# Inverse of the RWKV scores grown over all four 64x64 tiles, a bank for each row half

## The chip, the cores and the metric

The kernel runs on one core of one Trainium2 chip. The metric is the device time of one execution in microseconds (us). Before the change it is 1620.95 us, the median of three runs (1620.62 to 1621.21).

## The reference

Two layers of a hybrid decoder run over 256 prompt tokens and 64 sample tokens (8 sequences of 8). Each layer is a SwiGLU feed-forward block, a mixer of an RWKV-7 part (8 heads of 64) beside an mLSTM part (4 heads of 128), and a second feed-forward block, with a layer norm after each. The change is in the RWKV-7 part, whose step for one token is

```
def step(S, inp):
    r_t, w_t, k_t, v_t, kk_t, a_t = inp
    sa = jnp.einsum('bhvk,bhk->bhv', S, -kk_t)
    S = (S * w_t[:, :, None, :] + sa[..., None] * (kk_t * a_t)[:, :, None, :]
         + v_t[..., None] * k_t[:, :, None, :])
    return S, jnp.einsum('bhvk,bhk->bhv', S, r_t)
```

The kernel does this in chunks of 64 tokens. Inside a chunk the states depend on each other through a strictly triangular 64x64 matrix of scores for each head, and what is needed is the inverse of one plus that matrix. It then stands between the right-hand side and the vectors `u` that update the state and give the outputs.

## The kernel before

There are NCH = 5 chunks (4 of the prompt, 1 of all samples) and 8 heads. Heads lie in pairs: NJ = 4 pairs, of which one head is on partitions 0 to 63 and the other on 64 to 127 (`PART[0]`, `PART[1]`). A 64x64 matmul uses one of four tiles of TensorE, given by the row half its operands lie on and the half (columns of the array) its output goes to. A pair that stays on its half uses the two straight tiles; one that goes from `PART[q]` to `PART[1 - q]` uses the two crossed ones.

The inverse of a chunk is grown by doubling. `ati` holds one plus the scores. Level 0 masks it (on VectorE, into `xti` directly) and `first_growth` turns that into `xi`; TensorE then holds the inverse X and its transpose in `xx`, which lies in the space of `z`. Each later level of each chunk is one step n of a loop of NSTEP = 27 steps (six levels for a prompt chunk, three for the samples; the list `LEVELS` goes through the chunks level by level). Step n has four parts on three engines:

- `product(n)` on TensorE (L681): `ati` times X, 8 matmuls, into bank 0 or 1.
- VectorE (L1569): the product times the level's mask, into `t1`.
- `grow(n)` on TensorE, emitted one step later, after `product(n + 1)`: X times that (L693, 8 matmuls, not at a chunk's last level) and its transpose (L697, 8 matmuls), both into bank 2 or 3 by n, side by side. It waits for `t1`, and for the copy of the growth two back, which had the same bank.
- `copy_growth(n)` on ScalarE (L1073): the growth from its bank to `xx`, 128x512, or 128x256 where only one half is made.

These steps are the skeleton on which the rest of the mixer hangs. In steps of fixed numbers TensorE also does side work through bank 7 (`side`, with ScalarE's `copy_side`, each waiting for the one before): values (L627, copied at L1050), keys (L636, L643, copied at L1053, L1056), states (L656). It also does the mLSTM tiles: `tile_scores` in steps 9 and 14 (L527, L530), `tile_values` in steps 7 and 12 (L549 to L553), heads of the samples in steps 17 to 20 (L562 to L571), and left-overs from step 21 (L592, L428, L601). The order on every engine is written out by hand. Behind the loop, `recurrence` goes through the four prompt chunks with X transposed (L807), the products with the state (L794, L831) and the samples between. GpSimd makes a masked copy of the samples' keys for each pair in `memory_term` (L1741) for `samples_memory_after` (L775, L779); one of the four outputs lies in the gaps that `xx` leaves after the loop.

A fp32 matmul shows as two records in the trace, each with its weight load (PEld). The ends of matmul records are modelled; starts are what rests on firm ground.

## Time and profile before

| | |
|---|---|
| median of three runs | 1620.95 us |
| the profiled execution's own time | 1628.67 us |
| its span, from first to last instruction | 1626.9 us |
| PE busy | 1538.8 us, 95% |
| DVE, ACT, POOL busy | 845.4, 675.8, 373.9 us |
| mean granted clock | 0.965 |
| level loop of layer 0 | 399.4 to 488.9 us |
| level loop of layer 1 | 1201.0 to 1284.2 us |

PE is TensorE with its matmuls and PEld its weight loads, DVE is VectorE, ACT ScalarE, POOL GpSimd, SP the engine that issues DMAs. The granted clock is a share of 2.4 GHz; 0.50 is 1.2 GHz. In an order of time each row is a merged group: start, duration, engine, line, operation, output and inputs, shape, count, and in brackets how long the engine was idle before it and what ended that. "Issue" there is idle time for which the profile shows no release.

### The profile page before, as it was taken

The page shows a single profiled execution, that of the slowest core. Times are in us where ns is not written, and L with a number is a line of the kernel's source. Part 1 is how long each engine was busy: PE and PEld are TensorE (multiplying, and loading weights), DVE is VectorE, ACT ScalarE, POOL GpSimd, SP SyncE. Part 2 cuts the span into 40 slices and gives each one's busy share as a digit, 9 for nine tenths or more (in the row PEclk, how much of TensorE's full clock was granted, in tenths as well). Part 3 has the DMA queues.
Part 4 walks back from the last instruction along what each step waited for, and adds up shares of the span by engine and source line. Part 5 has one row for each costly group of instructions (what it writes and reads, how often), then busy time and mean ns, then how long its engine had stood idle before and what let it go on. Part 6 is the DMA issues. An engine that isn't in the chain of part 4 may idle for free.

```text
span 1626.9 us, 34539 instructions
## 1 busy us (share of the span) xinstructions
PE 1538.8 (95%) x13754; PEld 1478.2 (91%) x13754; DVE 845.4 (52%) x1333; ACT 675.8 (42%) x1111; POOL 373.9 (23%) x382
## 2 busy tenths in 40 slices
PE   7999998999998899999899999989999988999995
PEld 7999997998877899999899999979989777999994
DVE  4444345686265754444364443366954576444343
ACT  4333336656322453333353333367653245333332
POOL 6222460013112422221212221100131313222110
PEclk9999999999897999999999999999999899999998
DMA  7454542442112545454445454524430433545430
GB/s 204 144 154 143 166 146 79 125 112 77 29 44 73 173 131 153 145 151 143 135 117 154 144 153 156 142 79 117 104 81 3 116 97 112 169 145 154 144 115 33
DMA packets 307943, 197.73 MB, mean 122 GB/s; under 512 B 7616, under 2 KB 283104, under 8 KB 307840
## 3 DMA queue, kind: packets, MB, share of 16 engines
q1 hardware_dynamic: 304224, 189.64, 40.3%
q0 software_dynamic: 3616, 6.62, 1.6%
q8 instruction: 76, 1.25, 0.3%
q14 instruction: 27, 0.22, 0.0%
HBM read 187.46 MB, written 8.78 MB: 121 GB/s over the span
## 4 chain that ended last, share of the span: by engine, by line
PE 87%; DVE 5%; ACT 3%; DVEq 2%; issue 1%; POOL 1%; DMA 0%; ACTq 0%; SPq 0%; POOLq 0%
PE bank L1917 24%; PE bank L1918 23%; PE bank L1919 23%; PE bank L681 1%; PE bank L697 1%; PE bank L1960 1%; PE bank L592 1%; ACT x L2145 1%; PE bank L693 1%; DVEq L2284 1%; PE bank L568 1%; POOL xl L2387 1%; PE bank L429 1%; DVE xl L2275 1%; PE bank L1997 1%
## 5 line engine op out<-in xcount | busy, mean ns | idle before, releaser
L2243 DVE TENSOR_TENSOR wlo<-raw,whi 128x1024 fp32r<-128x1024 f32 x340 | 426.2, 1256 | 414.7 <-ACT whi L2121 413.5
L1917 PE MATMUL bank<-xh,whi 128*128 128x320 f32 x1896 | 591.3, 312 | 11.0 <-DVE wlo L2243 9.7
L2121 ACT ACTIVATE whi<-raw 128x1024 fp32r<-128x1024 f32 x340 | 359.0, 1059 | 571.3 <-PE bank L1919 565.8
L1918 PE MATMUL bank<-xl,whi 128*128 128x320 f32 x1896 | 588.0, 310 | 0.0
L1919 PE MATMUL bank<-xh,wlo 128*128 128x320 f32 x1896 | 587.9, 310 | 0.0
L1917 PEld LDWEIGHTS bank<-xh,whi 128*128 128x128 f32 x1896 | 357.7, 189 | 16.2 <-issue 6.2
L1918 PEld LDWEIGHTS bank<-xl,whi 128*128 128x128 f32 x1896 | 357.9, 189 | 0.5
L1919 PEld LDWEIGHTS bank<-xh,wlo 128*128 128x128 f32 x1896 | 357.8, 189 | 0.0
L2397 POOL TENSOR_TENSOR hl<-scratch,hh 128x320 f32 x88 | 146.6, 1666 | 529.1 <-DVE scratch L2308 529.1
L1917 PE MATMUL bank<-hh,whi 128*128 (+1 forms) x704 | 218.6, 310 | 0.7 <-ACT vec L2163 0.7
L1919 PE MATMUL bank<-hh,wlo 128*128 (+1 forms) x704 | 217.4, 309 | 0.0
L1918 PE MATMUL bank<-hl,whi 128*128 (+1 forms) x704 | 217.4, 309 | 0.0
L1917 PEld LDWEIGHTS bank<-hh,whi 128*128 128x128 f32 x704 | 132.3, 188 | 1.3 <-ACT vec L2163 1.0
L1918 PEld LDWEIGHTS bank<-hl,whi 128*128 128x128 f32 x704 | 132.3, 188 | 0.3
L1919 PEld LDWEIGHTS bank<-hh,wlo 128*128 128x128 f32 x704 | 132.3, 188 | 0.0
L2307 DVE TENSOR_TENSOR hh<-scratch,bank 128x320 f32 (+1 forms) x88 | 42.8, 487 | 122.5 <-PE bank L1919 121.0
L397 POOL TENSOR_TENSOR gbias<-ones 1x1 f32<-1x1 f32 x10 | 11.9, 1193 | 281.6 <-DVE scratch L1211 134.5
L1073 ACT ACTIVATE z<-bank 128x512 f32<-128x512 f32 (+1 forms) x54 | 27.8, 515 | 96.4 <-PE bank L697 96.4
L1960 PE MATMUL bank<-xh,whi 128*128 128x320 f32 x120 | 42.3, 360 | 26.9 <-ACT xh L2142 26.9
L1960 PEld LDWEIGHTS bank<-xh,whi 128*128 128x128 f32 x120 | 27.5, 229 | 28.6 <-issue 28.6
L2126 ACT ACTIVATE scratch<-z 128x320 f32<-128x320 f32 x48 | 20.4, 469 | 53.9 <-DVE z L2251 53.9
L2308 DVE TENSOR_TENSOR scratch<-scratch,bank 128x320 f32<-128x320 f32 x88 | 42.2, 479 | 0.0
(370 smaller groups left out, 1689.3 us busy)
## 6 DMA issues: line engine op xcount, KB each, us to landing
raw<-in_ffn_wg SPq DMA_DIRECT2D x88, 512.0 KB, 3.8
raw<-in_ffn_wu SPq DMA_DIRECT2D x88, 512.0 KB, 3.8
raw<-in_ffn_wd SPq DMA_DIRECT2D x88, 512.0 KB, 3.6
raw<-in_w_in SPq DMA_DIRECT2D x60, 512.0 KB, 3.8
raw<-in_w_out SPq DMA_DIRECT2D x16, 512.0 KB, 5.9
raw<-in_state_C SPq DMA_DIRECT2D x8, 512.0 KB, 6.0
out_s_C<-raw SPq DMA_DIRECT2D x8, 512.0 KB, 3.3
ring<-in_state_wkv POOLq DMA_DIRECT2D x2, 1024.0 KB, 8.7
```

Source lines behind the costliest of these rows:

```text
L429: return pe.matmul(out, src, ident[0:rows, 0:rows], start=True, stop=True)
L1073: act.activation(xx[:, c, lo:hi, :, :].rearrange("p x j s -> p (x j s)"), bank[2 + n % 2][:, lo * NJ * CH:hi * NJ * CH], ACT.Copy).then_in ...
L1917: pe.matmul(out, w_hi, hi, start=start, stop=False)
L1918: pe.matmul(out, w_hi, lo, start=False, stop=False)
L1919: return pe.matmul(out, w_lo, hi, start=False, stop=stop)
L1960: pe.matmul(outs[n], w[:, slot, k * P:(k + 1) * P], xh[:, k, :], start=(k == 0 and w is whi), stop=False)
L2121: act.activation(whi[:, slot, :], raw[:, slot, :], ACT.Copy).then_inc(hi_ready.sem, 1)
L2126: act.activation(sq[:, o, :], z[:, o, :], ACT.Square).then_inc(sq_ready.sem, 1)
L2243: dve.tensor_tensor(wlo[:, slot, :], raw[:, slot, :], whi[:, slot, :].bitcast(F32), ALU.subtract).then_inc(lo_ready.sem, 1)
L2307: dve.tensor_tensor(out, silu[:, s, :], bank[d % RS][:, 0:T], ALU.mult)
L2308: dve.tensor_tensor(hval[:, s, :], silu[:, s, :], bank[d % RS][:, 0:T], ALU.mult).then_inc(up_done.sem, 1)
L2397: pool.tensor_tensor(at(hl), hval[:, k % 2, :], at(hh).bitcast(F32), ALU.subtract).then_inc(hl_done.sem, 1)
```

## The change

The product now goes crossed, from the row half of the head to the other half (`PART[1 - q]`), so `t1` lies on the other half, and there the transposed inverse is kept too: `xi(q, c, j)` is on `PART[q]`, `xti(q, c, j)` on `PART[1 - q]`. A growth of both takes all four tiles: X goes crossed back, the transpose stays straight. What comes from row half 1 goes to bank 2, what comes from row half 0 to bank 3, at every level, so that `grow(n)` waits for the copy of growth n - 1. `first_growth` makes both X and its transpose, 16 matmuls in place of 8, and alternates between banks 2, 3 and banks 0, 1; the first product waits for the copy of growth 3. `copy_growth` takes two activations, one for each bank and head. What works with the transposed inverse in the recurrence takes its right-hand side on the other half, so the products that make it go crossed, and the side product RV goes straight. `memory_term` is two operations for each pair, and the output that lay in the gaps of `xx` has areas of its own.

```diff
-        xi, xti = xx[:, :, 0, :, :], xx[:, :, 1, :, :]
+        def xi(q, c, j):
+            return xx[PART[q], c, q, j, :]
+
+        def xti(q, c, j):
+            return xx[PART[1 - q], c, q, j, :]
...
-                        for q, part in enumerate(PART):
+                        for q in range(2):
                             at = (n * NJ + j) * NA
-                            last = pe.matmul(b[part, at:at + NA], scores[PART[1 - q], c, j, q, 0, :],
+                            last = pe.matmul(b[PART[1 - q], at:at + NA], scores[PART[1 - q], c, j, q, 0, :],
                                              uv[PART[1 - q], c, j, q, :], start=True, stop=True)
...
+        def growth_bank(n):
+            return 2 * ((n + 1) % 2) if n < NCH else 2
+
         def first_growth(pe, L, c):
 
             pe.wait_ge(t1_ready.sem, t1_ready.by(L, c + 1))
             if c >= 2:
                 pe.wait_ge(x_copied.sem, x_copied.by(L, c - 1))
             for j in range(NJ):
-                for part in PART:
-                    last = pe.matmul(bank[2 + c % 2][part, j * CH:(j + 1) * CH], xti[part, c, j, :],
-                                     ident[part, part], start=True, stop=True)
+                for q, part in enumerate(PART):
+                    pe.matmul(bank[growth_bank(c) + q][part, j * CH:(j + 1) * CH], t1[part, c, j, :], ident[part, part],
+                              start=True, stop=True)
+                for q, part in enumerate(PART):
+                    last = pe.matmul(bank[growth_bank(c) + q][PART[1 - q], j * CH:(j + 1) * CH], ident[part, part],
+                                     t1[part, c, j, :], start=True, stop=True)
             last.then_inc(x_mm.sem, 1)
 
         def product(pe, L, n):
 
             lv, c = LEVELS[n]
-            pe.wait_ge(x_copied.sem, x_copied.by(L, LEVELS.index((lv - 1, c)) + 1))
+            pe.wait_ge(x_copied.sem, x_copied.by(L, max(LEVELS.index((lv - 1, c)) + 1, NCH - 1)))
             pe.wait_ge(t1_ready.sem, t1_ready.by(L, n - 1))
             for j in range(NJ):
-                for part in PART:
-                    last = pe.matmul(bank[n % 2][part, j * CH:(j + 1) * CH], ati[part, c, j, :], xi[part, c, j, :],
+                for q, part in enumerate(PART):
+                    last = pe.matmul(bank[n % 2][PART[1 - q], j * CH:(j + 1) * CH], ati[part, c, j, :], xi(q, c, j),
                                      start=True, stop=True)
             last.then_inc(t1_mm.sem, 1)
...
             pe.wait_ge(t1_ready.sem, t1_ready.by(L, n + 1))
-            pe.wait_ge(x_copied.sem, x_copied.by(L, n - 1))
-            if lv < NLV[c] - 1:
-                for j in range(NJ):
-                    for part in PART:
-                        pe.matmul(bank[2 + n % 2][part, j * CH:(j + 1) * CH], xti[part, c, j, :], t1[part, c, j, :],
+            pe.wait_ge(x_copied.sem, x_copied.by(L, n))
+            for j in range(NJ):
+                if lv < NLV[c] - 1:
+                    for q in range(2):
+                        pe.matmul(bank[2 + q][PART[q], j * CH:(j + 1) * CH], xti(q, c, j), t1[PART[1 - q], c, j, :],
                                   start=True, stop=True)
-            for j in range(NJ):
-                for part in PART:
-                    last = pe.matmul(bank[2 + n % 2][part, (NJ + j) * CH:(NJ + j + 1) * CH], t1[part, c, j, :],
-                                     xti[part, c, j, :], start=True, stop=True)
+                for q in range(2):
+                    last = pe.matmul(bank[2 + q][PART[1 - q], j * CH:(j + 1) * CH], t1[PART[1 - q], c, j, :],
+                                     xti(q, c, j), start=True, stop=True)
             last.then_inc(x_mm.sem, 1)
...
             act.wait_ge(x_mm.sem, x_mm.by(L, n + 1))
-            lo, hi = int(lv == NLV[c] - 1), 1 + int(lv > 0)
-            act.activation(xx[:, c, lo:hi, :, :].rearrange("p x j s -> p (x j s)"),
-                           bank[2 + n % 2][:, lo * NJ * CH:hi * NJ * CH], ACT.Copy).then_inc(x_copied.sem, 1)
+            for q in range(2):
+                rows = slice(0, P) if lv < NLV[c] - 1 else PART[1 - q]
+                last = act.activation(xx[rows, c, q, :, :].rearrange("p j s -> p (j s)"), 
+                                      bank[growth_bank(n) + q][rows, 0:NJ * CH], ACT.Copy)
+            last.then_inc(x_copied.sem, 1)
...
-            if j == 1:
...
+            own = bcast(bmask[:, :].rearrange("p (b o) -> p b o", o=1), 2, NA)
+            for q in range(2):
+                src = bcast(bkt[NPC][:, j, q:q + 1, :], 1, SB)
+                last = pool.tensor_tensor(bktm[j][q], src, own, ALU.mult)
+            last.then_inc(memory_terms.sem, 1)
```

## Rows read from the trace of the kernel before

**Rows 1.** The page, busy time by engine.

```profile
PE 1538.8 (95%) x13754; PEld 1478.2 (91%) x13754; DVE 845.4 (52%) x1333; ACT 675.8 (42%) x1111; POOL 373.9 (23%) x382
```

**Rows 2.** Busy time by stretch: length, PE, PEld, DVE, ACT, POOL, clock, DMA share, GB/s.

```profile
399.40:488.90 89.50, 83.14 (x1709) 73.47 (x1707) 38.43 (x118) 32.77 (x76) 20.77 (x17) 0.90 0.14 36
1201.00:1284.20 83.20, 77.11 (x1709) 67.87 (x1707) 38.45 (x118) 32.74 (x77) 20.78 (x17) 0.98 0.15 39
...
421.00:423.00 2.00, 2.00 (x9) 1.78 (x9) 0.00 (x0) 0.00 (x0) 0.00 (x0) 0.50 0.00 0
```

**Rows 3.** PE in order of time, growth 6 of layer 1 (two tiles).

```profile
1212.04 0.63 PE L693 MATMUL bank<-spare,z 64*64 64x64 f32 x16
1212.50 0.63 PE L697 MATMUL bank<-z,spare 64*64 64x64 f32 x16
```

**Rows 4.** The scores: one group in order of time, and the line's durations (min/median/max).

```profile
388.36 1.10 PE L712 MATMUL bank<-scratch 64*64 64x128 f32 x32
...
L712 PE MATMUL bank<-scratch x320: 269/269/321, 388.4 to 1198.7; 64*64 64x128 f32 x160
```

**Rows 5.** PE in order of time, values (crossed) and first growth (straight), layer 1.

```profile
1203.63 0.51 PE L627 MATMUL bank<-ident,scratch 64*64 64x64 f32 x10 [0.99 <-ACT ring L1046]
1203.92 0.27 PE L670 MATMUL bank<-ident,z 64*64 64x64 f32 x2
1203.97 0.28 PE L627 MATMUL bank<-ident,scratch 64*64 64x64 f32 x3
...
1204.10 0.51 PE L670 MATMUL bank<-ident,z 64*64 64x64 f32 x11
```

**Rows 6.** Groups by line and shape, 395 to 520 us: count, busy, mean ns, idle before.

```profile
L1073 ACT ACTIVATE z<-bank 128x512 f32<-128x512 f32 x17 | 10.1, 597 | 39.0 <-PE bank L697 39.0
...
L1073 ACT ACTIVATE z<-bank 128x256 f32<-128x256 f32 x10 | 3.8, 375 | 11.5 <-PE bank L697 11.5
```

**Rows 7.** ACT in order of time in steps 5 and 6, and PE's L549 of step 7.

```profile
1211.74 0.77 ACT L1050 ACTIVATE scratch<-bank 64x256 f32<-64x256 f32 x2
1212.41 0.58 ACT L1073 ACTIVATE z<-bank 128x512 f32<-128x512 f32 x1
1213.18 0.60 ACT L1073 ACTIVATE z<-bank 128x512 f32<-128x512 f32 x1 [0.19 <-PE bank L697]
...
1213.07 1.16 PE L549 MATMUL bank<-ring 128*128 128x129 f32 x8
```

**Rows 8.** PE in order of time, the tile scores of step 9.

```profile
1218.93 2.02 PE L527 MATMUL bank<-scratch,sel 4*128 4x128 f32 x16 [0.41 <-DVE scratch L1352]
```

**Rows 9.** In order of time: the copy of growth 10 (ACT), and L549 of step 12.

```profile
1225.48 0.60 ACT L1073 ACTIVATE z<-bank 128x512 f32<-128x512 f32 x1 [0.99 <-PE bank L697]
...
1228.47 0.49 PE L549 MATMUL bank<-ring 128*128 128x129 f32 x2 [0.37 <-DVE ring L1339]
```

**Rows 10.** In order of time: L527 of step 14, and the copy of growth 15.

```profile
1235.46 1.97 PE L527 MATMUL bank<-scratch,sel 4*128 4x64 f32 x16 [0.24 <-DVE scratch L1354]
...
1241.02 0.60 ACT L1073 ACTIVATE z<-bank 128x512 f32<-128x512 f32 x1 [1.01 <-PE bank L697]
```

**Rows 11.** In order of time: the copy of growth 19, and L592 of step 21.

```profile
1255.83 0.60 ACT L1073 ACTIVATE z<-bank 128x512 f32<-128x512 f32 x1 [3.06 <-PE bank L697]
...
1261.91 1.95 PE L592 MATMUL bank<-spare,ring 64*128 64x512 f32 x4 [1.41 <-POOL spare L1729]
```

**Rows 12.** PE in order of time, growth 21 of layer 1.

```profile
1264.70 1.06 PE L693 MATMUL bank<-spare,z 64*64 64x64 f32 x16
1265.55 1.06 PE L697 MATMUL bank<-z,spare 64*64 64x64 f32 x16
```

**Rows 13.** PE in order of time, the first product of the recurrence.

```profile
1284.59 0.68 PE L807 MATMUL bank<-scratch,z 64*64 64x64 f32 x16 [0.48 <-ACT z L1073]
```

**Rows 14.** PE in order of time, inside growth 8 of layer 0.

```profile
418.25 0.38 PE L697 MATMUL bank<-z,spare 64*64 64x64 f32 x5 [1.17 <-issue]
```

**Rows 15.** PE in order of time, matmuls of 16 columns in the recurrence.

```profile
1287.51 3.99 PE L737 MATMUL bank<-scratch 64*64 64x16 f32 x128
```

More of the change, by code:

```diff
@@ L246, in hymba_kernel, with by_head @@
         decay = area(10504, SB, NJ, NA)
-        gaps = zflat.rearrange("p (c x r) -> p c x r", c=NCH, x=2)[:, 0:SB // 2, 0, :]
-        bktm_out = [area(2560, SB, P, of=spare), gaps.rearrange("p c (b n) -> p c b n", b=2),
-                    area(0, SB, P, of=spare), area(15304, SB, P)]
-        bktm = [[t[..., q * NA:(q + 1) * NA] for q in range(2)] for t in bktm_out]
+        def by_head(t):
+            return [t[..., q * NA:(q + 1) * NA] for q in range(2)]
+        bktm = [by_head(area(2560, SB, P, of=spare)), [area(20424, SB, NA), area(4314, SB, NA)],
+                by_head(area(0, SB, P, of=spare)), by_head(area(15304, SB, P))]
         wkv_out = area(5384, SB, NJ, NA)
@@ L744, in samples_r @@
             for j in range(NJ):
-                for part in PART:
-                    last = pe.matmul(bank[3][part, j * NA:(j + 1) * NA], s0sum[part, j, 0, :], ident[part, part],
-                                     start=True, stop=True)
+                for q, part in enumerate(PART):
+                    last = pe.matmul(bank[3][PART[1 - q], j * NA:(j + 1) * NA], s0sum[part, j, 0, :],
+                                     ident[part, part], start=True, stop=True)
             last.then_inc(samples_mm.sem, 1)
@@ L753, in samples_u @@
             for j in range(NJ):
-                for part in PART:
-                    last = pe.matmul(bank[3][part, j * NA:(j + 1) * NA], xti[part, NPC, j, :], rsb_s[part, j, :],
+                for q, part in enumerate(PART):
+                    last = pe.matmul(bank[3][part, j * NA:(j + 1) * NA], xti(q, NPC, j), rsb_s[PART[1 - q], j, :],
                                      start=True, stop=True)
@@ L792, in recurrence @@
                     for j in range(NJ):
-                        for part in PART:
-                            last = pe.matmul(bank[0][part, j * NA:(j + 1) * NA], ar[part, j, c, 0, :],
+                        for q, part in enumerate(PART):
+                            last = pe.matmul(bank[0][PART[1 - q], j * NA:(j + 1) * NA], ar[part, j, c, 0, :],
                                              state[part, c % 2, j, :], start=True, stop=True)
@@ L805, in recurrence @@
                 for j in range(NJ):
-                    for part in PART:
-                        last = pe.matmul(bank[1][part, j * NA:(j + 1) * NA], xti[part, c, j, :], rhs[part, j, :],
+                    for q, part in enumerate(PART):
+                        last = pe.matmul(bank[1][part, j * NA:(j + 1) * NA], xti(q, c, j), rhs[PART[1 - q], j, :],
                                          start=True, stop=True)
@@ L1562, in vector_mixers @@
                     dve.wait_ge(ati_ready.sem, ati_ready.by(L, c))
-                    tt(xti[:, c - 1, :, :], ati[:, c - 1, :, :], level_mask(0), ALU.mult).then_inc(t1_ready.sem, 1)
+                    tt(t1[:, c - 1, :, :], ati[:, c - 1, :, :], level_mask(0), ALU.mult).then_inc(t1_ready.sem, 1)
             for n in range(NCH, NSTEP):
@@ L1732, in memory_term @@
         def memory_term(pool, L, j):
-            if j == 1:
-                own = bcast(bmask[:, 0:SB].rearrange("p (c b o) -> p c b o", b=2, o=1), 3, P)
-                src = bkt[NPC][:, j, :, :].rearrange("p (o u q) n -> p o u (q n)", o=1, u=1)
-                src = bcast(bcast(src, 1, SB // 2), 2, 2)
-            else:
-                own = bcast(bmask[:, :].rearrange("p (b o) -> p b o", o=1), 2, P)
-                src = bcast(bkt[NPC][:, j, :, :].rearrange("p (o q) n -> p o (q n)", o=1), 1, SB)
-            pool.tensor_tensor(bktm_out[j], src, own, ALU.mult).then_inc(memory_terms.sem, 1)
+            own = bcast(bmask[:, :].rearrange("p (b o) -> p b o", o=1), 2, NA)
[3 more added lines that the diff above has]
+            last.then_inc(memory_terms.sem, 1)
         def pool_mixers(pool, L):
```

## The prediction

> **What bounds the kernel now.** I read the page first: TensorE (PE) is busy for 95% of the span [rows 1]. The change touches only one stage, so next I read the stretches of that stage, the level loop, once in each layer: 89.5 us in layer 0 and 83.2 us in layer 1, PE busy 93% in both, ACT 33 us and DVE 38 us [rows 2]. The same 27 steps take 6.3 us more in layer 0; the granted clock says why, 0.90 against 0.98, and a row inside layer 0 stands at 0.50, the 1.2 GHz level [rows 2]. The change of time is to be found in about 173 us of 1626.9, and at most what the grow groups take there. Third, I followed both loops in order of time, and wrote down at every idle piece of PE who released it. PE works through each step without a gap until it meets a wait that another engine ends: these places decide how much of a faster group is kept.
>
> **What a group costs.** With two tiles, a group of 8 fp32 matmuls of 64x64 leaves 16 records and its successor starts 0.47 us later, 29 ns a record [rows 3]. A full growth is two such groups, 0.93 us (L693 and L697); there are 17 of these in a layer (steps 5 to 13 and 15 to 22), and 5 last ones with one group.
>
> **Removed and added on PE.** The 17 full growths keep their 16 matmuls, but spread over all four tiles, one bank for each row half. Is that faster? The same layout runs in the scores at L712: 32 records of 128 columns in 1.10 us, one of them 0.269 us, so (1.10 - 0.27) / 31 = 27 ns a record, with four tiles of 107 ns each [rows 4]. Twice as many columns at the pace of two tiles: there four tiles do work twice as fast. With 64 columns the trace has only a short case: L627 (the crossed tiles) and L670 (the straight ones) follow each other, and L670 begins 0.29 us after L627 while 6 records of L627 are still to come; both are over in 0.75 us where 2 x 0.47 = 0.93 stood for two tiles, and in the overlapped piece some 11 records start in 0.18 us, 16 ns each [rows 5]. So 32 records cost between 32 x 14.5 = 0.46 us (half of 29) and 0.56 us (L627's own rate of 0.29 / 16 = 18 ns, if sending is the limit). I take 0.50, from the 16 ns: a full growth saves 0.43 us, bounds 0.37 to 0.47, where PE sets the time, and twice that at 1.2 GHz. The first growths go from 8 matmuls on two tiles to 16 on four: the same 0.47 to 0.50. Products, samples, recurrence and the RV side change only tiles: counts stay, I take zero; a short overlap with a neighbour, as in rows 5, could bring 0.1 us at each, half a microsecond in all.
>
> **Added on ACT.** One copy of 128x512 took 0.60 us and one of 128x256 0.38 [rows 6]. A full growth is now copied by two of 128x256: 0.77 us, as the pair at L1050 took [rows 7], so +0.17. A last growth goes from one copy (0.38) to two on one row half: +0.39. A first growth from one to two: +0.4. ACT gains 17 x 0.17 + 5 x 0.39 + 5 x 0.4 = 6.8 us a layer, and it has room in total (33 of 83). What counts is where a copy is waited for.
>
> **The added wait.** Growths of the levels no longer alternate between banks 2 and 3: both belong to each one, so the next growth waits for the copy of the one before (before, of the one two back). Behind the waiting growth stand, on PE, its side work, the next product and whatever tile work the step has. L697 of growth 6 starts at 1212.50 and its copy at 1213.18, 0.21 after the 0.47 of the group [rows 3, 7]. So from the end of a growth to the end of its copies it is 0.21 + 0.77, and with an estimated 0.06 for the signal back 1.04 us; the side group and the product between two growths give 0.94 with the clock up. Where a side group stands between, this is nearly hidden (0.1); in steps 6 and 8 there is none, and about 0.55 is waited.
>
> **The sum, layer 1, place by place.** (a) The first copy: L627 waits for L1046, which is behind the copy of growth 0 on ACT [rows 5]: +0.4. (b) Step 6: ACT comes late from its exponents to the copy of growth 5, at 1212.41 [rows 7]. Shifted by 0.4 and 0.77 long it ends at 1213.6; growth 6, which began at 1212.04 without it, now begins at 1213.65 and ends at 1214.15, and L549 starts at 1214.2 and not 1213.07: +1.1. Then growth 7 gains, growth 8 waits, and the next end is DVE's L1352, released by ACT's copy behind growth 7: L527 at 1218.93 [rows 8] becomes 1219.9. So (a) and (b) together: +0.95. (c) Steps 9 to 12: L549 waits for DVE, that for ACT's exponents, these for the copy of growth 10 [rows 9]. Growths 9 and 10 save 0.86, the two longer copies and the new wait take 0.4 back: -0.45; growth 11 gains nothing. (d) Steps 12 to 14: L527 at 1235.46 waits for DVE behind the copy of growth 12 [rows 10]: -0.43 + 0.17 = -0.25. (e) Steps 15 to 17: the copy of growth 15 at 1241.02 releases exponents and side copies [rows 10]; ACT is nearly full there, -0.1. (f) Steps 18 to 20: nothing waits between the long L568 groups, so growths 17, 18 and 19 save 1.29; then copy of growth 19, table load, roots, DVE, Pool and L592 at 1261.91 [rows 11], the copy +0.17: -1.1. DVE's head sums run beside it and end in time. (g) Growth 21 runs at the low clock, each of its groups 0.85 us apart [rows 12]: -0.86; growth 22 at full clock: -0.43. (h) After the last growth L807 waits for its copy [rows 13]: +0.4. Sum: 0.95 - 0.45 - 0.25 - 0.1 - 1.1 - 0.86 - 0.43 + 0.4 = -1.8 us.
>
> **Layer 0** has the same places and two differences. In growth 8 PE stood for 1.17 us with nothing to wait for [rows 14]; the delay of (b) falls into that gap, which is worth 0.9. And growths 9 and 10 ran mostly at 1.2 GHz [rows 2], so (c) is -1.0. Sum -1.8 - 0.9 - 0.55 = -3.3 us.
>
> Pool's four memory terms become two operations of 128x512 for one of 128x1024. PE uses them only in the fourth chunk of the recurrence and after it, behind three chunks of other work: nothing; without that cover it would be about 4 x 0.2 us, what a halved copy cost more on ACT [rows 6, 7]. Nothing else of SP's or Pool's queue moves. Together -5.1 us, so the profiled span goes from 1626.9 to 1621.8. The profiled execution's own time was 1628.67, 7.7 over the median of the runs; I take the same difference from the median: 1620.95 - 5.1 = 1615.8 us.
>
> **A rule that speaks against it.** In the overlap of L627 and L670 tiles of the same row half loaded and multiplied in turns, and each kept its pace [rows 5]. The Trainium skill, "TensorE: Matmul & The Clock Gate", Part 3, The mechanism, says that a weight load overlaps a running matmul only when the row group differs; with it the two tiles of a row half would go one after the other. It is the third rival below; the trace so far disagrees, but over 6 records only.
>
> **Rivals.** First, the clock turns against it. In layer 0 a stretch from 420.7 to 427.4 us stood at half clock (one slice of it is in the rows), and layer 1, at 0.98 in all, had none in those steps [rows 2]. PE does the same work in less time and waits more in steps 6 and 8, so a further stretch of that kind may fall in; 6.7 us at half clock cost 3.3: -5.1 + 3.3 gives 1619, within 0.2%. The same the other way: the stretch of layer 0 goes, -3.3 more and 0.6 less to gain there: 1613. Second, the new wait costs more than I give it, by 0.3 us at each of the 7 neighbouring growths without long work between them, twice: +4.2 gives 1620, no change. Third, the one that ends slower: four tiles go no faster than two with 64 columns, because loading or sending 30 ns a record is the floor. For it speaks L737, whose matmuls have 16 columns and not 64, and which still took 3.99 us for 128 records, 31 ns each [rows 15]; that is a floor for each tile (61 ns) or for all of them, and the row does not tell which. Against it speak rows 4 only in part (27 ns is also just what 128 columns need) and rows 5. Then a growth stays at 0.93 and only costs are left: (b) +1.8, (c) +0.4, (d) +0.2, (e) +0.3, (f) +0.2, (h) +0.4, 3.3 in layer 1, and 0.9 less in layer 0: 5.7, which gives 1626.6. From 1615.8 that is 10.8 us, the 0.43 of some 25 growths' worth on the path (12 in layer 1, 13 in layer 0, one at half clock counted twice). So it decides from 5.1 / 25 = 0.20 us a growth, 32 x 6.4 ns: above 22 ns a record nothing is gained.
>
> **How the numbers follow.** Forecast 1615.8 with its own range 1613.5 to 1618 (0.37 or 0.47 for each of the 25 is 1.5 up or 1.0 down, the small overlaps 1 down, layer 0's gap 0.9 up): 0.40. Clock in its favour: 0.12. Clock against: 0.22. Wait dearer: 0.12. Four tiles no faster: 0.14. A measurement of this kernel can tell about 0.2% (3.2 us) from no change, so faster means under 1617.7. Forecast (nine tenths of it) and good clock give 0.48 + 0.02 from the rest; slower is the third rival and a little of a bad clock: 0.16; same: 0.34. The range leaves out most of the third rival and the ends of the clock cases: 1611.5 to 1622.
>
> **What would show it.** The growth lines: 32 records in 0.6 to 0.7 us at full clock with the next group 0.50 us after the start, not 0.93. L1073 twice as often, 128x256. A wait of PE for L1073 before growths 6 and 8, about 0.5 us each. L549 of step 7 a good 1 us later counted from the first L627; L592 about 1.2 earlier than without that. The wait before L807 0.4 longer. The two level loops together 5 us shorter, everything behind them as before. It is wrong if the records of a growth start 27 to 30 ns apart, or if the clock row of the loops differs by more than 0.03 from 0.90 and 0.98.

## The result

The changed kernel took 1629.1 us in the median of 18 executions (1618.4 to 1632.6), the kernel before 1622.3 (1620.6 to 1625.4, 18 executions): a ratio of 1.0034, interval 1.0023 to 1.0044. It is slower, by about a third of a per cent, where 5 us less had been forecast, and it lies above the range. Two things stand beside this from the start. The spread became three times as wide (14 us for 5), and the time follows the mean granted clock: from 1618.4 us at 0.969 to 1632.6 at 0.956. The first profiled execution was by chance the fastest of the 18; a second profile, of a repeat of the same kernel, is a typical one at 1628.8 us. Both are needed: the first shows what the change does where the clock is at 2.4 GHz, the second what it costs. The kernel before was repeated and profiled again too; that profile, 1619.25 us, is 2.6 under the median of its repeat.

| | before, rows of the section above | before, repeated | after, first profile | after, repeated |
|---|---|---|---|---|
| profiled execution, us | 1628.67 | 1619.25 | 1618.43 | 1628.84 |
| span, us | 1626.9 | 1617.5 | 1616.7 | 1627.1 |
| mean granted clock | 0.965 | 0.972 | 0.969 | 0.959 |

The page of the changed kernel, first profile: busy time by engine, and the copies of the growths. PE has lost 15 us of busy time against [rows 1] (part of it clock), ACT has gained 8.

```profile
PE 1523.3 (94%) x13914; PEld 1461.7 (90%) x13914; DVE 844.6 (52%) x1333; ACT 684.2 (42%) x1165; POOL 376.3 (23%) x390
...
L1085 ACT ACTIVATE z<-bank 128x256 f32<-128x256 f32 (+1 forms) x108 | 36.3, 379 | 81.2 <-PE bank L708 80.9
```

**What a growth costs now.** PE in order of time, first profile, layer 1, step 19: a product (L693), growth 18 (L705 straight, L708 crossed) and the head sums behind it. This answers to [rows 3].

```profile
1238.47 0.33 PE L693 MATMUL bank<-z,spare 64*64 64x64 f32 x4
...
1238.64 0.46 PE L693 MATMUL bank<-z,spare 64*64 64x64 f32 x10
1238.89 0.27 PE L708 MATMUL bank<-z,spare 64*64 64x64 f32 x2
1238.93 0.23 PE L693 MATMUL bank<-z,spare 64*64 64x64 f32 x2
1238.99 0.22 PE L705 MATMUL bank<-spare,z 64*64 64x64 f32 x2
1239.00 0.23 PE L708 MATMUL bank<-z,spare 64*64 64x64 f32 x2
1239.05 0.23 PE L705 MATMUL bank<-spare,z 64*64 64x64 f32 x2
...
1239.40 0.68 PE L642 MATMUL bank<-ident,spare 64*64 64x64 f32 x16
```

Two records of L705 and two of L708 start every 0.055 to 0.06 us, about 14.5 ns each, and the whole of product and growth takes 1239.40 - 1238.47 = 0.93 us, the time that a growth alone took. With 0.46 for the product the growth is 0.47: the better end of my bounds, 0.46 to 0.56.

**What PE waits for.** The same view, layer 1, the waits of the stage that bear on the sum; they answer to [rows 5, 8, 9, 10, 11, 13].

```profile
1196.04 0.51 PE L633 MATMUL bank<-ident,scratch 64*64 64x64 f32 x10 [1.24 <-ACT ring L1057]
...
1205.60 0.27 PE L705 MATMUL bank<-spare,z 64*64 64x64 f32 x2 [1.28 <-ACT z L1085]
...
1210.25 0.27 PE L705 MATMUL bank<-spare,z 64*64 64x64 f32 x2 [0.42 <-ACT z L1085]
...
1211.73 0.46 PE L533 MATMUL bank<-scratch,sel 4*128 4x128 f32 x2 [0.32 <-DVE scratch L1365]
...
1221.99 0.49 PE L555 MATMUL bank<-ring 128*128 128x129 f32 x2 [0.37 <-DVE ring L1352]
...
1228.62 1.63 PE L533 MATMUL bank<-scratch,sel 4*128 4x64 f32 x13 [0.29 <-DVE scratch L1367]
...
1253.15 1.95 PE L598 MATMUL bank<-spare,ring 64*128 64x512 f32 x4 [1.95 <-POOL spare L1742]
...
1273.30 1.01 PE L818 MATMUL bank<-scratch,z 64*64 64x64 f32 x13 [0.87 <-ACT z L1085]
```

Two waits are new, before growths 6 and 8 (1.28 and 0.42 us, both for the copy of the growth before), and three have grown: before the first values 1.24 for 0.99 [rows 5], before the first left-over group 1.95 for 1.41 [rows 11], before the first product of the recurrence 0.87 for 0.48 [rows 13].

**Where the time went.** The stage cut at these instructions. The us at half clock of a stretch (its time at the 1.2 GHz level) are 2 x (1 - granted clock) x its length. "Clock up" is a stretch without any: for before from its repeat (the last full-clock one, 21.24, from a version described below), for after from the first profile, from the layer that had none. The last row has half clock in every profile, given behind its lengths.

| stretch | before, clock up | after, clock up | difference | after, repeated, layer 1 (us at half clock) |
|---|---|---|---|---|
| first values to L549/L555 of step 7 | 9.44 | 10.19 | +0.75 | 10.18 (0) |
| to the tile scores of step 9 | 5.86 | 5.50 | -0.36 | 5.50 (0) |
| to L549/L555 of step 12 | 9.54 | 8.87 | -0.67 | 10.22 (3.5) |
| to the tile scores of step 14 | 6.99 | 6.63 | -0.36 | 6.64 (0) |
| to the first left-over group | 26.45 | 24.53 | -1.92 | 25.32 (3.5) |
| to the first product of the recurrence | 21.24 | 20.15 | -1.09 | 24.74 (10.4) |
| to the first matmul of the next stage | (40.69, 13.8 low) | (40.92, 13.9 low) | +0.2 | 41.72 (16.7) |

With +0.25 ahead of the first values, a layer is 3.4 us shorter as long as the clock is up, nearly twice what I had expected (1.8). The last column is what a typical execution makes of it. Three stretches of layer 1 (the level loop from the first values up to the left-overs, from there to the recurrence, the recurrence) in both repeats; columns: length, PE, PEld, DVE, ACT, POOL, granted clock, DMA share, GB/s. First the kernel before:

```profile
1194.15:1252.43 58.28, 53.28 (x1305) 50.50 (x1305) 21.74 (x60) 24.84 (x57) 13.04 (x13) 1.00 0.09 22
1252.43:1275.13 22.70, 22.22 (x370) 16.18 (x371) 15.50 (x54) 5.64 (x13) 5.50 (x3) 0.92 0.31 90
1275.13:1315.82 40.69, 34.67 (x731) 29.17 (x731) 25.69 (x60) 10.93 (x22) 9.91 (x9) 0.83 0.26 72
```

The changed kernel:

```profile
1201.12:1258.98 57.86, 51.05 (x1353) 47.56 (x1353) 21.42 (x59) 27.52 (x77) 12.77 (x13) 0.94 0.10 22
1258.98:1283.72 24.74, 23.87 (x370) 16.32 (x371) 15.62 (x54) 7.16 (x19) 5.50 (x3) 0.79 0.28 82
1283.72:1325.44 41.72, 35.23 (x731) 29.43 (x731) 24.79 (x60) 10.93 (x22) 10.68 (x13) 0.80 0.26 71
...
1262.00:1264.00 2.00, 2.00 (x37) 1.50 (x30) 0.60 (x3) 0.98 (x4) 1.00 (x1) 0.50 0.03 8
```

PE has the same 370 records in the middle stretch, with 10.4 us at 1.2 GHz for 3.6. The first profile has this stretch with the clock up throughout:

```profile
1253.15:1273.30 20.15, 19.28 (x371) 13.42 (x371) 15.49 (x54) 7.16 (x19) 5.52 (x3) 1.00 0.35 100
```

So here 10.4 us at half clock cost 24.74 - 20.15 = 4.6 us, 0.44 us for each. Over a whole execution the second profile of after has 2 x 0.041 x 1627 = 133 us at half clock, the first 100; that of before, repeated, has 2 x 0.028 x 1617.5 = 91, and its first one 114. So two executions of one kernel give a price over the whole program: 10.4 us of span for 33 us at half clock in the changed kernel, 9.4 for 23 in the kernel before, 0.3 to 0.4 us for each.

### The profile page after: what moved, and what is told of

Its sections match the earlier page's. It is cut to its first block, busy times and chain, and to the rows that moved or that the text cites. A ratio compares the mean times of both kernels' runs of the same rounds, so it can differ in the third digit from the quotient of the medians.

```text
span 1616.7 us, 34921 instructions
## 1 busy us (share of the span) xinstructions
PE 1523.3 (94%) x13914; PEld 1461.7 (90%) x13914; DVE 844.6 (52%) x1333; ACT 684.2 (42%) x1165; POOL 376.3 (23%) x390
## 4 chain that ended last, share of the span: by engine, by line
PE 87%; DVE 5%; ACT 4%; DVEq 2%; issue 1%; POOL 1%; DMA 0%; ACTq 0%; POOLq 0%
PE bank L1927 24%; PE bank L1928 24%; PE bank L1929 24%; PE bank L1970 1%; PE bank L693 1%; PE bank L598 1%; ACT x L2155 1%; DVEq L2294 1%; PE bank L574 1%; PE bank L705 1%; POOL xl L2397 1%; PE bank L435 1%; DVE xl L2285 1%; PE bank L2007 1%; DVE z L2276 1%
## 5 line engine op out<-in xcount | busy, mean ns | idle before, releaser
L1085 ACT ACTIVATE z<-bank 128x256 f32<-128x256 f32 (+1 forms) x108 | 36.3, 379 | 81.2 <-PE bank L708 80.9
```

The lines of the kernel that those rows point to most:

```text
L1085: last = act.activation(xx[rows, c, q, :, :].rearrange("p j s -> p (j s)"), bank[growth_bank(n) + q][rows, 0:NJ * CH], ACT.Copy)
```

## The experiments

The theory after the first profile: the change does what it should at full clock, but it makes PE's idle pieces in this stage longer, more of the stage then runs at 1.2 GHz, and this takes more than the growths give. The rival: the waits and copies cost it by themselves. All versions ran beside the kernel before, whose median was 1623.4, 1622.2 and 1623.0 us in the three groups of four.

**The two kernels again.**

> The changed kernel again, unaltered, with the kernel before on the same chip. Clock theory (the level loops got shorter, but more of the execution runs at 1.2 GHz): its executions spread from about 1618 to 1632 us in step with their mean granted clock, about 1.2 us for each 0.001; at equal clock it lies some 5 us under the kernel before; a profile of a slow execution shows level loops of 77 to 80 us where the clock is up, and stretches at 0.50 that the fast one hasn't. Cost theory (the bank wait and the longer copies cost more than the tiles give): the time does not follow the clock, and slow executions have longer waits of PE for L1085 at full clock.

> The kernel before as a run of its own, for its clock beside its times. Clock theory: its executions stand at 0.963 to 0.966 and 1620.5 to 1626 us, and a change of clock moves it by the same 1.2 us for each 0.001. Cost theory: the clock is that of the changed kernel, and the times differ all the same.

After: 1628.9 us (1620.4 to 1634.4, 12 executions), ratio 1.0031 (1.0012 to 1.0051). Before: 1621.9, ratio 0.9998 (0.9986 to 1.0010). The loss is real, and what this measurement tells apart is about 0.2%. Of the 12 executions of after the nine at a clock of 0.962 or less took 1626 to 1634 us, the other three, at 0.964 to 0.968, 1620.4 to 1621.8. The kernel before stood at 0.966 to 0.973, higher than I had written. At nearly equal clock the changed kernel is ahead, as the clock theory has it: its six executions at 0.964 and 0.965 took 1620.4 to 1624.7 us, the five of the kernel before at 0.966 took 1625.0 to 1628.6 (all runs together). The mean clock does not fix the time alone: at 0.971 the kernel before took from 1620.3 to 1625.1 us.

**The growth without the turns.** The changed kernel, all straight matmuls of a growth sent ahead of the crossed ones (the expectation has the two the other way round; the edit is this one):

```
-            for j in range(NJ):
-                if lv < NLV[c] - 1:
+            if lv < NLV[c] - 1:
+                for j in range(NJ):
                     for q in range(2):
                         pe.matmul(bank[2 + q][PART[q], ...
+            for j in range(NJ):
                 for q in range(2):
                     last = pe.matmul(bank[2 + q][PART[1 - q], ...
```

> Changed kernel, but in a growth the crossed half (8 matmuls) is sent as a whole before the straight half, as before the change; layout, banks, waits and copies stay. Clock theory: the growth takes 0.8 to 0.93 us again, each level loop is 3 to 5 us longer at full clock, PE is busier and the granted clock steadier, near 0.965: about 1625. Cost theory: 8 to 10 us slower than the changed kernel, about 1638, since only costs are left. Prediction's pace theory (four tiles no faster than two): no change from the changed kernel.

1629.9 us, ratio 1.0051 (1.0034 to 1.0067): 5 us over what the clock theory gave and 8 under the cost theory, so neither number came. PE in order of time, layer 1, a growth with the clock up:

```profile
1243.29 0.51 PE L705 MATMUL bank<-spare,z 64*64 64x64 f32 x10
1243.58 0.27 PE L709 MATMUL bank<-z,spare 64*64 64x64 f32 x2
1243.60 0.28 PE L705 MATMUL bank<-spare,z 64*64 64x64 f32 x3
```

Alone, ten records of L705 take 0.29 us, 29 ns each; the crossed ones start only then, as in [rows 5]. Stretches with one full growth at full clock (to the tile scores of steps 9 and 14) are 5.76 and 6.89 us for 5.50 and 6.63, so a growth comes to 0.73 us here and not 0.47: the turns are worth 0.26 us each, an estimated 34 times 0.26 = 8.8 us of PE time over both layers. The median moved by 1 us, the ratio by 0.2%, and the intervals overlap. Most of PE's gain is therefore not in the result. A place where it goes stands in the same trace: the slower growths bring PE later to the first left-over group, and it waits 1.51 us there, not 1.95; behind it the clock stays up (the same in layer 0, 20.81 us at 1.00):

```profile
1262.61 1.95 PE L598 MATMUL bank<-spare,ring 64*128 64x512 f32 x4 [1.51 <-POOL spare L1743]
```

```profile
1262.61:1283.40 20.79, 19.92 (x370) 14.06 (x371) 15.49 (x54) 7.15 (x19) 5.51 (x3) 1.00 0.34 97
```

Some of the gained time turns into idle time of PE there. In the second profile of the changed kernel the wait that is 0.44 us longer stands ahead of a stretch that is 4 us longer, by its half clock. The length of the wait alone does not decide this: 1.95 us were followed by none in the first profile of the changed kernel, and the shorter 1.41 us of the kernel before by 3.4 us at half clock in each layer of both its profiles. And this version has its half clock elsewhere: 2 x 0.035 x 1625.9 = 114 us in all, of which 7 (layer 0) and 10 (layer 1) lie between the first values and the tile scores of step 14, where the second profile of the changed kernel has 7 and 3.4.

**The costs without the gain.** The kernel before, with the changed kernel's wait and its copies in two activations, and then with the copies alone. The full edit:

```
-            pe.wait_ge(x_copied.sem, x_copied.by(L, n - 1))
+            pe.wait_ge(x_copied.sem, x_copied.by(L, n))
 ...
-            act.activation(xx[:, c, lo:hi, :, :]..., bank[2 + n % 2][:, lo * NJ * CH:hi * NJ * CH], ACT.Copy)
+            for q in range(2):
+                x0, x1, rows = (q, q + 1, slice(0, P)) if hi - lo == 2 else (lo, hi, PART[q])
+                last = act.activation(xx[rows, c, x0:x1, :, :]..., 
+                                      bank[2 + n % 2][rows, x0 * NJ * CH:x1 * NJ * CH], ACT.Copy)
```

> Kernel before, with the two costs alone: a growth waits for the copy of the growth just before it, and each copy is two activations. Clock theory: +2 to +3 us a layer by the sum (wait in steps 6 and 8, later exponents, later u), about 1627, with the clock within 0.002 of before. Cost theory: +5 us a layer and more, 1632 and up.

> The kernel before with each growth's copy in two activations, but with the wait of before (for the copy of two growths back). The version with the new wait as well was at 1640.9 us, 1.012 of before. Theory (the wait carries most of the loss when growths are not faster): 1624 to 1630 us, so that the wait alone is 11 us or more. Rival (ScalarE's longer copies carry it): 1634 us or more.

Both together: 1640.9 us, ratio 1.0117 (1.0098 to 1.0135), 4 executions; the clock theory had said 1627, the cost theory 1632 and more. The copies alone: 1633.9, ratio 1.0077 (1.0058 to 1.0095), also 4, at the edge of what the rival asked for, where I had said 1624 to 1630. In both the rival's number held and mine did not: the copies carry some 12 us and the wait some 7, where my ledger had the costs of both at 5.7 us together. What remained to settle is by what way they cost so much. The copies alone are the clearest case, since they hardly lengthen anything by themselves. Groups by line and shape of that version, 395 to 520 us, where its copies stand in both shapes:

```profile
L1075 ACT ACTIVATE z<-bank 128x256 f32<-128x256 f32 x34 | 11.2, 382 | 36.1 <-PE bank L697 36.0
L1075 ACT ACTIVATE z<-bank 64x256 f32<-64x256 f32 x20 | 7.5, 375 | 10.7 <-PE bank L697 10.6
```

ACT in order of time, one such pair:

```profile
1214.70 0.66 ACT L1075 ACTIVATE z<-bank 128x256 f32<-128x256 f32 x2 [1.09 <-PE bank L697]
```

A pair of 128x256 is over in 0.66 us where one 128x512 took 0.60 [rows 6], and a first or last copy (two of 64 rows) in 0.76 for 0.38. In its profile the stretch from the first scores to the start of the next stage is 140.4 and 141.5 us in the two layers, against 135.3 in both of the kernel before: 11.3 of the 13.6 us by which the two spans differ. Pieces with equal half clock show the copies' own cost: ahead of the first values 14.19 us for 13.66, from step 12 to 14 7.05 for 6.99, from there to the left-overs 26.57 for 26.45, from these to the recurrence 23.06 for 22.70 (some 3.4 us at half clock in both), 1.1 us a layer. And 27 and 31 us of these stretches are at half clock, against 17 and 17: 24 us more, which at 0.3 to 0.44 are 7 to 11 of the 11.3. The first values waited 1.52 us for 0.99 there, and in layer 1 10.2 us at half clock followed, where before had none:

```profile
1202.09 0.51 PE L627 MATMUL bank<-ident,scratch 64*64 64x64 f32 x10 [1.52 <-ACT ring L1046]
```

So the two theories were not as separate as I had put them: the copies do cost 12 us, and most of it by way of the clock. The version with both costs shows how loosely a single wait and the clock hang together: in its profile L592 waits 1.48 us in both layers, and the stretch behind is 27.83 us at 0.75 in layer 0 and 23.08 at 0.93 in layer 1. Against this version the changed kernel is 12 us faster (1640.9 to 1628.9), which the new layout as a whole brings; the turns alone brought 1 to 3 of it.

**Filling one idle piece.** The changed kernel with four matmuls that nobody reads, just ahead of the first left-over group:

```
+        def filler(pe, b, times):
+            for _ in range(times):
+                pe.matmul(b[:, 0:4 * CH], ident[:, :], lvmask[:, 0:4, :], start=True, stop=True)
 ...
+                if n == LEFT_AT[0]:
+                    filler(pe, bank[(n - 1) % 2], 4)
```

> The changed kernel with four matmuls more in each layer, 128x128 by 256 columns, sent to an idle bank just before the first left-over group (L598), where TensorE stood idle for 1.95 us; their result is overwritten and never read, so they are extra work of about 1.7 us laid into that idle piece. Theory (the change is faster at full clock, and loses by longer stretches at half clock that follow its idle pieces): the 10.4 us at half clock between L598 and the first samples group L818 go, that stretch falls from 24.8 to between 20.2 and 22 us in each layer, and the whole comes to 1620 to 1624 us against 1629 without the extra matmuls. Rival (the added costs are the waits and copies themselves, and the clock falls elsewhere anyway): no gain, 1629 or up to 1632 us, with the stretch still at 24 us or the same time at half clock found in its neighbours.

1618.0 us (1614.9 to 1621.0, 11 executions), ratio 0.9972 (0.9960 to 0.9983): 11 us less than the changed kernel (by the ratios 10), for 8 x 0.43 = 3.4 us of extra work (two records a matmul, one started every 0.216 us). PE in order of time, layer 1:

```profile
1253.15 0.63 PE L649 MATMUL bank<-scratch 64*64 64x64 f32 x16
1253.71 1.99 PE L868 MATMUL bank<-lvmask,ident 128*128 128x256 f32 x8
1255.73 1.95 PE L598 MATMUL bank<-spare,ring 64*128 64x512 f32 x4
```

The piece of 1.95 us is filled (L868 stands as 8 records for 4 matmuls), L598 begins no later (6.14 us behind the copy of growth 19 in both versions), and the stretch behind it is as short as in the fastest execution, at full clock:

```profile
1255.73:1275.89 20.16, 19.29 (x371) 13.42 (x371) 15.50 (x54) 7.14 (x19) 5.51 (x3) 1.00 0.36 100
```

The time is better than the 1620 to 1624 expected. Twice 4.6 us are these stretches; the remaining 1.7 of the 11 I can't place.

**The same on the kernel before** (three matmuls ahead of L592).

> The kernel before with three such extra matmuls at the same place (idle there 1.41 us), results never read. It tells whether the extra matmuls are worth something by themselves. Theory: in the kernel before the stretch from L592 to L807 has only 3.4 us at half clock in each layer, so at most 1.8 us a layer is to be had: 0 to -3.5 us. If it gains as much here as on the changed kernel, what they give is not a debt of the change.

1619.4 us, ratio 0.9985 (0.9973 to 0.9996): 2.8 us less. The stretch fell from 22.70 to 21.24 in each layer and had nothing at half clock, the value used in the table above. The same cure brings four times as much on the changed kernel, so most of what it brings there, 8 of the 11 us, is a debt of the change.

**The control.** The same four matmuls on the changed kernel, two steps earlier, where PE has no idle piece (`if n == LEFT_AT[0] - 2`).

> A control: the changed kernel with the same four extra unread matmuls a layer as in the version that came to 1618.0 us, but two steps earlier, where TensorE has no idle piece. Theory (they help only where they fill an idle piece): no gain, 1629 to 1633 us, their own 1.7 us a layer being added. Rival (any extra work there holds the clock up): under 1625 us.

1632.5 us, ratio 1.0043 (1.0023 to 1.0062). PE in order of time, layer 1:

```profile
1263.14 1.09 PE L598 MATMUL bank<-spare,ring 64*128 64x512 f32 x2 [1.95 <-POOL spare L1749]
```

The stretch from there to the recurrence:

```profile
1263.14:1287.88 24.74, 23.87 (x370) 16.29 (x371) 15.61 (x54) 7.16 (x19) 5.50 (x3) 0.79 0.29 82
```

The wait of 1.95 us is there as in the changed kernel, and behind it the same 24.74 us at 0.79; in layer 0 it is 26.37 us at 0.74. Extra work alone gains nothing here and adds its own length; the gain needs it in the idle piece. Four of its 10 executions, at 0.964 to 0.968, took 1622.4 to 1625.8 us, the other six 1632.3 to 1636.2: the spread of the changed kernel is still there, while the 11 executions with the piece filled lie within about 6 us.

**More fillings**: two and one ahead of growths 6 and 8, two ahead of the recurrence's first product, four ahead of the samples' solution (L766), on top of the four; and for comparison the kernel before with three ahead of L592 and the two and the four in the recurrence.

```
+                    if n in (NCH + 2, NCH + 4):
+                        pe.wait_ge(t1_ready.sem, t1_ready.by(L, n))
+                        filler(pe, bank[(n - 1) % 2], 2 if n == NCH + 2 else 1)
 ...
                 if c == 0:
+                    filler(pe, bank[1], 2)
 ...
                     if c == 2:
+                        filler(pe, bank[7], 4)
                         samples_u(pe, L)
```

> warm21 with more of the same extra matmuls where the changed kernel waits or stands idle: two before growth 7's neighbour in the first level, one two steps later, two ahead of the first solution of the recurrence, four before the samples' solution; none is read. Theory: the time at half clock in the level loop and in the recurrence falls too, 1612 to 1619 us. Rival (each extra matmul delays the wait's end or the work behind it, since the pieces are only 0.4 to 1.3 us long): 1620 to 1628 us, slower than warm21.

> The kernel before with extra unread matmuls in the same places as the changed kernel's best version as far as it has them: three ahead of L592, two ahead of L807, four ahead of the samples' solution. It tells what the grow groups are worth with the idle pieces of both kernels filled. Theory: 1614 to 1618 us, so that the changed kernel (1616.0) is ahead by 0 to 2 us only. If it comes to 1620 or more, the change is worth over 4 us once its clock is held.

1616.0 us, ratio 0.9963 (0.9949 to 0.9977), and 1618.1, ratio 0.9968 (0.9957 to 0.9979). The second steps brought 2.0 and 1.3 us: most was in the one piece. Over all five versions with the piece filled, the stretch from the left-overs to the recurrence stands at 1.00 in both layers, ten of ten. With both kernels' idle pieces filled the intervals overlap: the change is then worth 2 us by the medians, 1 by the ratios, and not surely anything.

**One copy for both banks.** The changed kernel, with banks laid out in pairs, so that one activation copies both:

```
-            for q in range(2):
-                rows = slice(0, P) if lv < NLV[c] - 1 else PART[1 - q]
-                last = act.activation(xx[rows, c, q, :, :]..., bank[growth_bank(n) + q][rows, 0:NJ * CH], ACT.Copy)
+            last = act.activation(xx[:, c, :, :, :]...,
+                                  pair[growth_bank(n) // 2][:, :].rearrange("p (x r) -> p x r", x=2)[:, :, 0:NJ * CH],
+                                  ACT.Copy)
```

> The changed kernel, but both banks of a growth are copied in one activation (128 rows, two pieces of 256 columns from two neighbouring banks) instead of two. The waits and TensorE's work stay. Theory (the second activation lengthens the waits ahead of growths 6 and 8, of L818 and of the roots before L598, and TensorE's clock falls after them): a copy takes 0.60 us and not 0.77, a last copy and a first one no more than 0.6, the waits before growths 6 and 8 shrink from 1.28 and 0.42 us to about 1.0 and 0.2, and the whole falls by several times the 0.17 us of each place: 1617 to 1624 us against 1629. Rival (the copies cost only their own length where they are waited for, about 0.17 at five places and 0.4 at three, in two layers): -4 us, 1625 to 1627.

> One copy for a growth as in the run before, with the extra unread matmuls of the version that came to 1616.0 us. Theory (both cures act on the same thing, the pieces in which TensorE stands idle, so their gains overlap in part): 1606 to 1614 us, faster than the kernel before and than either cure alone. If it stays at 1616 the single copy gives nothing once the idle pieces are filled.

Alone 1625.5 us (12 executions, 1615.6 to 1627.5), ratio 1.0003 (0.9987 to 1.0020): 3.4 us less than the changed kernel (by the ratios 4.5), the rival's figure and not mine. The copy is 0.59 us long, but the pair had been over in 0.63 to 0.66, so there were only 0.06 us to be had at the waits before the first values, growths 6 and 8 and the left-overs; before the recurrence, where the last copies had taken 0.77, the wait fell from 0.87 to 0.70. Groups of this version by line and shape, 395 to 520 us:

```profile
L1084 ACT ACTIVATE z<-pair 128x512 f32<-128x512 f32 x27 | 16.0, 593 | 45.0 <-PE pair L709 44.9
```

PE in order of time, its wait before the first left-over group:

```profile
1254.23 1.09 PE L599 MATMUL pair<-spare,ring 64*128 64x512 f32 x2 [1.89 <-POOL spare L1742]
```

The idle piece is 1.89 us, and 24.6 us with 10.3 at half clock follow as before. With the fillings as well: 1610.5 us (1608.6 to 1611.7, 6 executions), ratio 0.9922 (0.9910 to 0.9934), the fastest version, 12.5 us under the kernel before, at a clock of 0.975 in its profile. Its level loop and the stretch behind it in layer 1:

```profile
1190.22:1246.52 56.30, 53.38 (x1367) 48.74 (x1367) 21.53 (x59) 26.12 (x57) 12.83 (x13) 0.97 0.10 23
1246.52:1266.80 20.28, 20.28 (x376) 14.10 (x375) 15.50 (x54) 6.39 (x13) 5.78 (x4) 1.00 0.35 101
```

The time lies within the 1606 to 1614 expected. Why one copy gives another 5.5 us on top of the fillings, more than the 3.4 it gives alone, no single place shows; the two profiles differ by 3.1 us.

## Why the prediction was wrong

**The pace of four tiles: right.** 0.47 us for a growth, the better end of the bounds (0.46 to 0.56, 0.50 taken). The third rival (no faster than two tiles) is out; that its 1626.6 us is the number of mine nearest to the result is luck. The Trainium skill says in "TensorE: Matmul & The Clock Gate", Part 3, The mechanism, that a weight load overlaps running matmuls only where the row group differs. This trace disagrees: straight and crossed tiles of one row half take turns at 14.5 ns a record against 29 for two tiles alone, so a row half starts a record every 29 ns, where with two tiles, one in each row half, it started one every 58. They do so only if sent in turns, as the version without turns shows with 0.73 us.

**The copies: the size was off, in their favour, in the ledger.** A pair of 128x256 takes 0.63 to 0.66 us and not the 0.77 I took from a pair of 64 rows; so (a) was +0.25 and not +0.4. Only the last copies, two of 64 rows, took the 0.77. ACT's busy time rose by 8.4 us over both layers, 4.2 a layer, where 6.8 had been added up.

**The places: right in sign, mostly too small.** (a) and (b) to the tile scores of step 9: +0.64 measured (0.25 + 0.75 - 0.36), 0.95 forecast. (c) -0.67 for -0.45; (d) -0.36 for -0.25; (e) and (f) -1.92 for -1.2; (g) and (h) -1.09 at full clock, where the forecast of -0.89 had 0.43 from half clock in it. In all -3.4 us a layer for -1.8 in layer 1. The waits before growths 6 and 8 were forecast at about 0.5 each and were 1.28 and 0.42; that for growth 6 was contained in the start I gave for it (1213.65 - 1203.63 - 0.4 = 9.62 us behind the first values, measured 9.56; for L549 of step 7 10.17, measured 10.19), so "about 0.5" contradicted my own ledger, and (b) itself was right.

**The step that failed: the clock was taken as given.** I priced each wait and each longer copy at its own length and laid the profile's clock over the result. The version with the costs alone measures this step: 5.7 us in my ledger, 18.7 in the medians. The first rival named the right mechanism and the right steps (the waits in steps 6 and 8), but put it at one further stretch of 6.7 us, 3.3 us of time, with a chance of 0.22. In fact the second profile has some 42 us more at half clock than the repeat of the kernel before (133 for 91), nearly all in this stage: in the level loop, behind it and in the recurrence. At 0.3 to 0.44 us each, an estimate from the stretches and spans above, these are 13 to 18 us; the two profiles need 16.4 (6.8 us gained at full clock, 9.6 lost between 1619.25 and 1628.84), the medians 13.7. The kernel before has such executions too: that of the rows had 114 us at half clock, most of the surplus in layer 0, and took 1628.67; in the changed kernel this became the usual case. The sign that I gave, a clock of the loops more than 0.03 from 0.90 and 0.98, did come: cut as in [rows 2], up to the recurrence, they stand at 0.88 and 0.90 in the second profile (86.1 and 85.0 us), against 0.98 in both layers (83.1 us) in the repeat of the kernel before. In the first profile they are 80.2 and 79.7 us at 0.96 and 0.98.

**A sum that hid it.** In (f) I counted 1.1 us of gain ahead of L592, and never asked what becomes of the wait there. The chain of copy, roots, DVE and Pool takes 6.14 us from the copy of growth 19 to L598, for 6.08 before; growth 20 lies beside that chain, so what it saves moves nothing and only brings PE to the wait earlier, and the idle piece grows from 1.41 [rows 11] to 1.95 us. That one piece, filled, gives back 11 us, where the whole loss is 7. A faster engine that still waits for the same chain has a longer idle piece as its first result.

**What stays open.** Which idle piece is followed by half clock is not fixed: in the first profile the same wait of 1.95 us before L598 was followed by 20.15 us at full clock, in both layers, and 1.51 us by none where 1.41 and 1.48 were followed by some. The runs show that filling one such piece, or making the copies longer, moves the time by 11 or 12 us; they don't give a rule for a single piece, nor for what in an execution decides it. Which of the longer pieces costs how much, other than the one before the left-overs, was not measured one by one. That the copies cost 12 us in the kernel before while one copy for two gave only 3.4 in the changed one is of the same kind.

## What to carry to other kernels

On an engine with a granted clock, a wait is not worth its length alone: write down, place by place, how long PE stands idle before and after the edit, and treat longer pieces as a possible cost of their own, which here came to several times their length in most of the profiles. Before judging a change that makes PE faster between two waits, put unread matmuls into the longest idle piece of both kernels and compare again, with a control where the engine is busy: here the verdict went from 0.3% slower to level, and with one copy for two to 0.5% faster. And compare several executions with their clocks, not one profile: the first profile of the changed kernel was its fastest execution and showed the opposite of the median.

## What the runs showed of the hardware

- Four tiles of 64x64 with 64 columns start a record every 14.5 ns (0.47 us for 32), with straight and crossed tiles sent in turns; sent one kind after the other, the first ten start 29 ns apart and the growth takes 0.73 us.
- Records of the growth (L708 at 1238.89) start before the last ones of the product sent ahead of them (L693 at 1238.93).
- Two activations of 128x256 behind each other end after 0.63 to 0.66 us, one takes 0.38, and one of 128x512 0.59; one activation can read two neighbouring banks at that price.
- Behind the idle piece ahead of the left-over groups the granted clock fell to the 1.2 GHz level or not, and not in order of the piece's length. 1.95 us: none of the next 20.15 us in both layers of the first profile, 10.4 us of the next 24.7 in both of the repeat and in layer 1 of the control, 13.7 in layer 0 of the control. 1.89 us (one copy): 10.3 us in both layers. 1.51 us (no turns): none in both. 1.48 us: 3.2 us in three stretches of the two versions with longer copies, 13.9 in the fourth. 1.41 us (kernel before): 3.4 to 3.6 us in all four. Filled with three or four unread matmuls: none in ten of ten.
- Each us at half clock cost 0.44 us in the stretch where PE was 96% busy, and 0.3 to 0.4 between two whole executions of one kernel.
